# A router with stationary weights, a gather from the norm's weighted rows, and low parts made by GpSimd

## What is computed

```python
x = layer_norm(ALPHA * x + h, ln_g[i, 0], ln_b[i, 0])     # h: output of the windowed attention
logits = (xf @ w_router).astype(jnp.float32)              # 256 x 8
top_val, top_idx = lax.top_k(logits, TOP_K)               # 2 of 8 experts
top_w = jax.nn.softmax(top_val, axis=-1)
for e in range(N_EXPERTS):
    h = jax.nn.silu(xf @ w_gate[e]) * (xf @ w_up[e])      # 1024 x 3584
    out = out + gates[:, e:e + 1] * (h @ w_down[e])
```

## Time and profile before

| | us |
|---|---|
| median of 3 runs | 2149.47 |
| lowest and highest | 2147.61, 2150.2 |
| the profiled execution, its own time | 2145.25 |
| span of its profile | 2143.4 |
| granted TensorE clock, mean | 0.995 |
| TensorE busy | 2104.2 |
| VectorE busy | 1755.8 |
| ScalarE busy | 1508.5 |
| GpSimd busy | 397.3 |

### The profile page before, as it was taken

One profiled execution on the slowest core, in us unless ns is written; L12 is line 12 of the kernel. 1 busy time (PEld: TensorE's weight loads), 2 busy tenths in 40 slices (PEclk: granted clock), 3 DMA queues, 4 the chain that ended last, 5 costly groups with the idle time before them and its releaser, 6 DMA issues.

```text
span 2143.4 us, 32785 instructions
## 1 busy us (share of the span) xinstructions
PE 2104.2 (98%) x12715; PEld 1820.4 (85%) x12715; DVE 1755.8 (82%) x2194; ACT 1508.5 (70%) x2018; POOL 397.3 (19%) x354
## 2 busy tenths in 40 slices
PE   9999999989999999999999999999999999999998
PEld 8888888878888888888888888888899888999887
DVE  6756766879999999999999999986699676689775
ACT  5644444666887888888888888876578955668964
POOL 1511000001002000000000000000558700277820
PEclk9999999999999999999999999999999999999999
DMA  8225956439999999999999999994656465655561
GB/s 286 100 66 130 278 183 181 162 100 353 361 361 387 394 387 394 380 391 365 395 360 395 378 382 375 382 361 134 203 164 205 153 233 164 190 179 176 179 211 60
DMA packets 297418, 564.58 MB, mean 263 GB/s; under 512 B 19600, under 2 KB 113576, under 8 KB 297256
## 3 DMA queue, kind: packets, MB, share of 16 engines
q1 hardware_dynamic: 285328, 527.60, 69.7%
q0 software_dynamic: 11824, 34.77, 5.9%
q10 hardware_dynamic: 104, 0.04, 0.0%
HBM read 548.32 MB, written 14.02 MB: 262 GB/s over the span
## 4 chain that ended last, share of the span: by engine, by line
PE 92%; DVE 4%; ACT 2%; issue 1%; SPq 1%; DMA 0%; DVEq 0%; ACTq 0%
PE bank L953 26%; PE bank L955 26%; PE bank L954 25%; PE bank L1549 4%; PE bank L959 2%; PE bank L1550 2%; PE bank L1953 1%; PE bank L1130 1%; DVE parts L2857 1%; PE bank L1913 1%; PE bank L1934 0%; PE bank L1926 0%; DMA raw<-in_a_w_in_dram 0%; DVE work L2996 0%; PE bank L1876 0%
## 5 line engine op out<-in xcount | busy, mean ns | idle before, releaser
L2857 DVE TENSOR_TENSOR parts<-raw,parts 128x1024 fp32r<-128x1024 f32 x701 | 849.8, 1228 | 274.6 <-ACT parts L2086 249.5
L2086 ACT CAST parts<-raw 128x1024 fp32r<-128x1024 f32 x701 | 730.8, 1048 | 395.3 <-PE bank L955 313.9
L2857 DVE TENSOR_TENSOR fast<-raw,fast 128x1024 fp32r<-128x1024 f32 x302 | 361.9, 1218 | 24.2 <-ACT fast L2086 7.4
L2086 ACT CAST fast<-raw 128x1024 fp32r<-128x1024 f32 x302 | 316.4, 1052 | 84.6 <-PE bank L955 78.1
L953 PE MATMUL bank<-parts,cols 128*128 128x512 f32 x868 | 344.2, 397 | 3.2 <-DVE cols L2911 1.9
L955 PE MATMUL bank<-parts,cols 128*128 128x512 f32 x868 | 338.5, 390 | 0.0
L954 PE MATMUL bank<-parts,cols 128*128 128x512 f32 x868 | 338.2, 390 | 0.0
L953 PE MATMUL bank<-cols,parts 128*128 128x256 f32 x1040 | 300.4, 289 | 0.0
L954 PE MATMUL bank<-cols,parts 128*128 128x256 f32 x1040 | 294.8, 283 | 0.0
L955 PE MATMUL bank<-cols,parts 128*128 128x256 f32 x1040 | 294.8, 283 | 0.0
L953 PEld LDWEIGHTS bank<-cols,parts 128*128 128x128 f32 x1040 | 199.3, 192 | 4.0 <-issue 2.0
(11 more groups left out here) (457 smaller groups left out, 3454.1 us busy)
## 6 DMA issues: line engine op xcount, KB each, us to landing
raw<-in_moe_w_gate_dram SPq DMA_DIRECT2D x112, 1024.0 KB, 9.4
raw<-in_moe_w_up_dram SPq DMA_DIRECT2D x112, 1024.0 KB, 8.9
raw<-in_moe_w_down_dram SPq DMA_DIRECT2D x112, 1024.0 KB, 9.2
raw<-in_w_in_dram SPq DMA_DIRECT2D x76, 1024.0 KB, 5.4
raw<-in_a_w_in_dram SPq DMA_DIRECT2D x11, 1024.0 KB, 11.7
raw<-in_ffn_w_gate_dram SPq DMA_DIRECT2D x11, 1024.0 KB, 5.5
raw<-in_ffn_w_up_dram SPq DMA_DIRECT2D x11, 1024.0 KB, 5.5
raw<-in_ffn_w_down_dram SPq DMA_DIRECT2D x11, 1024.0 KB, 5.0
```

The lines of the kernel that those rows point to most:

```text
L2086: a.copy(dst[0], src).then_inc(*up(o + "hi", x))
L2857: v.tensor_tensor(dst[1], src, dst[0].bitcast(F32), ALU.subtract).then_inc(*up(o + "lo", x))
```

## The change

1. The router's weights become the stationary operand: high and low parts lie side by side in one slot (16 columns for each of the 8 blocks of the width), and the tokens move, high and low parts in one matmul of 256 columns. That is 8 matmuls for each tile, into banks 5 and 0. The result has the experts on the partitions. VectorE copies it to SBUF, and TensorE turns it with two small float32 products for each tile, with a 16 x 8 matrix `fold` that also adds the high and low rows; VectorE copies that to the logits.
2. The gather of expert 0 reads P, not X. The selection matrix for it holds 1/deviation in place of 1 (`sel_sd`, `spots`), so it waits for the counts and for nothing of the norm's rows; the norm's offset is transposed into the gather's two banks ahead of time (8 transposes). Banks 4 and 6 are taken.
3. The counts are three products in place of five, and three float32 products of the identity, written to bank 1 and read by nobody, stand before `sel` and behind the counts (`keep_busy`).
4. The norm's rows are written by VectorE within the norm: tile 1's right behind its diagonal, tile 0's behind tile 1's low parts.
5. The low parts of eight weight pieces (the five late ones, `GATE_LO`, and the three behind the router's, `ROUTE_LO`) are GpSimd's. GpSimd takes the three after its four DMAs of X, and loads the next norm's constants only when the gather is done, since their buffer now lies where P does.
6. On VectorE the two low parts of the gather come before `route_ends`; `picked(0)` and `ids(0)` move from expert step 0 to step 1.

```diff
+    GATE_LO = LATE_LO[2]
+    ROUTE_LO = list(W.after.get(T_rt, ()))
...
+        for y in GATE_LO:
+            piece_lo(y)
         gp.wait_ge(*at("rows", 2, 0))
         gp.wait_ge(*at("lo_x", 2, 0, 1))
         for d in (x_d, f_d):
             gp.dma_start(d[0:T, :].rearrange("(a p) d -> p a d", p=128), X).then_inc(*up("x_away", 0, by=16))
             gp.dma_start(d[T:, :], X[:, 0, :]).then_inc(*up("x_away", 0, by=16))
+        for y in ROUTE_LO:
+            piece_lo(y)
+        gp.wait_ge(*at("gathered", 0, 1))
         ln_rows(N4.gb, 1, 1, 3)
...
-        narrow(bank[5], T_rt, 8, 5, TILES[2], 2)
-        busy[5] = ("logits",)
+        def logits():
+            pe.wait_ge(*at(lo_name(T_rt), T_rt))
+            both = v3(router_slot(), 8)
+            for t, b in zip(TILES[2], (5, 0)):
+                claim(b)
+                pe.wait_ge(*at("lo_x", 2, t, 1))
+                o = bank[b][0:16, 0:T].rearrange("p (q c) -> p q c", q=2)
+                for k in range(8):
+                    k_ = pe.matmul(o, both[:, k, :], v3(XT_both[:, k, :], 2)[:, :, t * 128:(t + 1) * 128], start=k == 0, stop=k == 7, skip_group_check=True)
...
+            for t in TILES[2]:
+                pe.wait_ge(*at("logit_rows", t))
+                for q in range(2):
+                    k_ = pe.matmul(bank[7][:, 32 + 8 * t:40 + 8 * t], N4.lT[:, t * T + q * 128:t * T + q * 128 + 128], N4.fold, start=q == 0, stop=q == 1)
+            k_.then_inc(*up("logits_turned"))
+        logits()
+
+        for hf in range(2):
+            b = gather_bank(MAIN, 0, hf)
+            claim(b)
+            for j in range(4):
+                cs = slice((4 * hf + j) * 128, (4 * hf + j + 1) * 128)
+                pe.matmul(bank[b][:, j * 128:(j + 1) * 128], N3.gb[:, 1, cs], ident, start=j == 0, stop=False, is_transpose=True, skip_group_check=True)
+        claim(1)
+        keep_busy(3, 1, ident)
         pe.wait_ge(*at("sel"))
...
+                if e == 0 and o == MAIN:
+                    pe.wait_ge(*at("spots"))
+                    for j in range(4):
+                        kk = 4 * hf + j
+                        for t in range(2):
+                            k = pe.matmul(bank[b][:, j * 128:(j + 1) * 128], N3.P[:, t, kk * 128:(kk + 1) * 128], N4.P_[:, 1, t, :], start=False, stop=(j, t) == (3, 1), skip_group_check=True)
...
-                if i == 0:
-                    for y in rest[:between]:
-                        lo(W, MAIN, y)
-            del rest[:between]
+                if n == 2 and i == 0:
+                    norm_rows(n, gb, P, (t,))
             for i, t in enumerate(TILES[n]):
                 for g in range(2):
                     cols_lo(n, XT, t, g, 6 + g - 2 * t)
                 for y in (rest[:1], rest[1:])[i]:
                     lo(W, MAIN, y)
+                if n == 2 and i == 0:
+                    norm_rows(n, gb, P, TILES[n][1:])
...
-        norm_rows(2, N3.gb, N3.P)
+        v.tensor_tensor(N4.sel_sd, sel[:, :, 0:1], v3(LT[:, 0:16], 2)[:, :, 5:6], ALU.mult).then_inc(*up("dve"))
+        v.wait_ge(*at("dve"))
         v.wait_ge(*at("counts"))
+        for t in range(2):
+            k = v.tensor_scalar(N4.P_[:, 1, t, :], C(C_IOTA), bank[7][:, 8 * t:8 * t + 1], N4.sel_sd[:, t, :], ALU.is_equal, ALU.mult)
+        k.then_inc(*up("spots"))
...
             picks(0)
+            gather(0, 0)
+            gather(0, 1)
             if side:
                 route_ends()
-                for y in rt_next[:3]:
-                    lo(W_, o, y)
-            gather(0, 0)
-            if side:
-                for y in rt_next[3:]:
-                    lo(W_, o, y)
-            gather(0, 1)
```

More of the change, by code:

```diff
@@ L84 @@
     "dve_merge": ("yb", "merged"),
-    "dve_expert": ("picks", "lo_g", "hh", "lo_h", "y", "sum", "ids"),
+    "dve_expert": ("spots", "picks", "lo_g", "hh", "lo_h", "y", "sum", "ids"),
     "dve_o_expert": ("o_picks", "o_lo_g", "o_hh", "o_lo_h", "o_y", "o_sum"),
@@ L431, in _program @@
         pass
-    N4.gb = v3(take(2 * D), 2)
-    N4.fa = v3(take(2 * D), 2)
-    N4.xg = [tuple(v3(cols_[:, q, 1024 * a:1024 * a + 1024], 8) for q in range(2)) for a in range(2)]
-    sg_hh = take(4 * 512)
-    N4.sg, N4.hh = v3(sg_hh[:, 0:1024], 2), v3(sg_hh[:, 1024:2048], 2)
     N4.P_ = v4(take(2 * 256), 2, 2)
@@ L442, in _program @@
     N4.ids = take(2).bitcast(U32)
+    N4.gb = v3(take(2 * D), 2)
+    N4.fa = v3(take(2 * D), 2)
+    N4.xg = [tuple(v3(cols_[:, q, 1024 * a:1024 * a + 1024], 8) for q in range(2)) for a in range(2)]
+    sg_hh = take(4 * 512)
+    N4.sg, N4.hh = v3(sg_hh[:, 0:1024], 2), v3(sg_hh[:, 1024:2048], 2)
+    N4.lT = sg_hh[0:16, 0:512]
     N4.rows, N4.ys = N4.fa[:, 0, :], N4.fa[:, 1, :]
@@ L452, in _program @@
     N4.left = v4(rt[:, 192:224], 2, 2)
+    N4.fold, N4.sel_sd = rt[0:16, 32:40], v3(rt[:, 40:42], 2)
     N4.g01 = v3(rt[:, 128:132], 2)
@@ L683, in raw_view, with router_slot @@
         return raw[:, c % RAW, 0:a * b].rearrange("p (a b) -> p a b", a=a)
+    def router_slot():
+        i = W.pieces[T_rt]["slot"]
+        return (parts_[:, i, 0, :] if i < PIECES else more[i - PIECES])[:, 0:128]
     def piece_view(W_, x):
@@ L688, in piece_view @@
         i = W_.pieces[x]["slot"]
+        if W_ is W and x == T_rt:
+            return src, tuple(v3(router_slot(), 8)[:, :, 8 * q:8 * q + 8] for q in range(2))
         if i >= PIECES:
@@ L694, in _program, with gather_bank @@
     MAIN, MORE = "", "o_"
+    def gather_bank(o, e, hf):
+        if o == MAIN and e == 0:
+            return (4, 6)[hf]
+        return 6 if (e, hf) == (0, 1) else 7
     def sync_program(sp):
@@ L1706, in tensor_program @@
-        pe.matmul(bank[7][:, 16:24], ones, sel[:, 1, :], start=False, stop=True).then_inc(*up("counts"))
+        def logits():
[7 more added lines that the diff above has]
+                    k_ = pe.matmul(o, both[:, k, :], v3(XT_both[:, k, :], 2)[:, :, t * 128:(t + 1) * 128], start=k == 0, stop=k == 7, skip_group_check=True)
+                k_.then_inc(*(up("logit_cols", t) if t == TILES[2][0] else up("used", T_rt)))
+                busy[b] = ("logit_rows", t)
+            claim(7)
+            for t in TILES[2]:
[3 more added lines that the diff above has]
+            k_.then_inc(*up("logits_turned"))
@@ L1707, in tensor_program @@
+        pe.matmul(bank[7][:, 8:24], ones, sel[:, 0, :].unsqueeze(1).broadcast_to([128, 2, 8]), start=False, stop=False, skip_group_check=True)
+        pe.matmul(bank[7][:, 16:24], ones, sel[:, 1, :], start=False, stop=True, skip_group_check=True).then_inc(*up("counts"))
+        keep_busy(3, 1, ident)
         busy[7] = ("ranked",)
@@ L2860, in after @@
             for y in W_.after.get(x, ()):
-                if W_ is W2 or y not in late and y not in POOL_LO:
+                if W_ is W2 or y not in late and lo_name(y) == "lo":
                     lo(W_, o, y)
@@ L2919, in norm_rows, with residual_norm @@
                 k.then_inc(*up("rows", n, t))
-        def residual_norm(n, gb, P, ends, x_in=None, between=0):
-            rest = list(LATE_LO[n])
+        def residual_norm(n, gb, P, ends, x_in=None):
+            rest = list(LATE_LO[n]) if n < 2 else []
             if n == 0:
@@ L3500, in experts @@
                     gather(e + 1, g - 4)
-                if side and n == 0:
+                if side and n == 1:
                     ids(0)
```

63 lines of the change are left out of this document (34 added, 29 removed).

## The result

The changed kernel takes 2160.21 us (median of 7 runs, 2155.88 to 2162.58) against 2147.61 us of the kernel before (7 runs beside it). By the medians it is 12.6 us slower; the ratio is 1.0053 [1.0041, 1.0064], which is 11.4 us. Forecast were 0.9 us faster, and 2152.5 was the upper end of the range. The profiled execution took 2160.21, span 2158.3.

A forecast was written before the change was run, and what follows sets the result against it. TensorE, busy 98%, bounds the kernel, so only the 19.57 us ahead of the experts can shrink: 7.2 us gained less 6.3 lost to GpSimd overlap is 0.9, from 2149.47 to 2148.6 us; range 2142.0 to 2152.5.

The forecast's parts named there:

- Norm held by GpSimd: Third norm: VectorE's ln_p and diagonal wait for GpSimd's pieces, so TensorE's tile 0 starts 5.4 us later.
- half clock on tile 0's 16 instructions: Norm on TensorE: half clock behind the idle gap, on about half of the 16 instructions, loses 0.9 us.
- Router: Router up to the logits: 16 matmuls of 256 columns in place of 32 narrow ones, gain 1.3 us.
- Norm rows off the selection: Selection to gather: without the norm rows on VectorE the counts come last, gain 2.6 us.
- Gather at full clock and nothing late behind it: Expert 0's gather: 3.6 us against 6.25, gain 2.65; low part of its first half no longer late, gain 0.6.
- Sum of the gains: Router, selection, gather and what follows it: 7.2 us together, first gate product at 486.3 before losses.
- Small instructions of the selection beside GpSimd: Selection's 8 to 16 column VectorE instructions: taken as 0, though up to 2.3 us for each one caught.
- margin of 0.4 us: Selection: spots due at 488.6, GpSimd's ROUTE_LO at about 489; 0.4 us later and spots is held.
- rivals, 2: Selection: ROUTE_LO holds spots and picks, 2 or 3 times 2.3 us on top; 2153.2 to 2155.5 us, chance 0.12.
- sign against the clock step: Gather: if it takes over 5 us, the claim of 3.6 us at clock 1.00 is wrong.
- The prediction's own rule: VectorE beside GpSimd: two SBUF operands, or a wide SBUF-to-SBUF instruction, wait until GpSimd's running instruction ends.
- GpSimd's pieces were never late: Weights: GpSimd's pieces slow but not late; a TensorE wait for a weight piece after 493 us would refute it.

The follow-up runs named there:

- e8_gaps: Changed kernel with three norm low parts on GpSimd behind tile 0's diagonal, two on VectorE, norm rows later, ROUTE_LO on VectorE: 2147.22 us, ratio 0.9986.
- e6_route_late: Changed kernel plus one wait: GpSimd starts ROUTE_LO only when expert 0's selection (picks) is written; 2148.27 us, ratio 0.9999.
- e11_early_picks: e8_gaps with picks(1), expert 1's selection, moved right behind route_ends on VectorE; 2146.56 us, ratio 0.9985.
- e1_vector_lows: Changed kernel with all eight low parts given back to VectorE, the rest of the change kept; 2150.21 us, ratio 1.0001.
- e3_route_vector: Changed kernel with ROUTE_LO given back to VectorE and GATE_LO kept on GpSimd; 2148.56 us, ratio 1.0001.
- e10_no_filler: e3_route_vector without the two groups of three idle identity products (keep_busy) around the counts; 2150.58 us, ratio 1.0011.
- e5_before_gpsimd: Kernel before with only the eight low parts moved to GpSimd, router, gather and norm rows as before; 2160.67 us, ratio 1.0054.
- base_again: Meant as a second profile of the kernel before; by mistake the changed kernel ran unaltered; 2155.98 us (one run).

## Why the prediction was wrong

Step by step, with the measured value behind the predicted one:

- Norm held by GpSimd: 5.4 predicted, 8.51 - 3.63 = 4.9 measured; half clock on tile 0's 16 instructions 0.9 predicted, measured about 1.6 (483.22 to 486.62, against 1.78). The mechanism and the instructions (second half of `ln_p`, diagonal) are those named.
- Router: gain 1.3 predicted. In `e8_gaps`, where hardly anything is held, B is 6.22 against 6.87; with the step that the kernel before still needs behind its copy, some 0.9. In `e6_route_late` B is 7.18; without the 1.6 of half clock this is 5.6, a gain of 1.3.
- Norm rows off the selection: 2.6 predicted, 4.07 - 1.62 = 2.45 measured in `e6_route_late`.
- Gather at full clock and nothing late behind it: 2.65 + 0.6 = 3.25 predicted, 6.90 - 3.59 = 3.31 measured in the same kernel. There the clock did stay up. In the changed kernel it fell to 0.50 at 494.3, in the wait for held instructions, and E is 5.12.
- Sum of the gains: 7.2 predicted, 5.4 in the stretch of `e8_gaps`, where the clock stays up. The prediction also let every microsecond at the first gate product arrive at the end; in `e8_gaps` and `e11_early_picks` 1.9 and 1.7 of it were given back by 660 us. This term was mis-sized, but it isn't what put the time outside the range.
- Small instructions of the selection beside GpSimd: taken as 0. **This is the step that failed.** C and D are 5.33 + 5.34 in the changed kernel and 1.78 + 1.62 in `e6_route_late`, which differs by one wait: 7.3 us. E adds 1.5 through the clock, B 0.3. That is 9.1 of the 9.5 us between the two profiles' spans (2158.3 and 2148.8). The medians of the two lie 11.9 us apart; the rest isn't traced to anything.
- Behind the first gate product the changed kernel falls back by another 1.95 us against the kernel before, up to 1879 us. Up to 1440 us it is 0.9, without any wait, and the same 0.9 to 1.0 is in `e1_vector_lows`, `e3_route_vector`, `e6_route_late` and `e10_no_filler`, whatever their start; `e5_before_gpsimd`, with the old router and gather, has none. So it comes with the rest of the change and not with GpSimd. No run tells from which part; the prediction had no term for it.

The prediction's reason for the 0 was that piece 5 and the DMAs lie beside most of the selection. This place was right: logits to `ROUTE_LO` were 2.8 us in the forecast and are 493.49 - 490.68 = 2.81. But it took DMA issues as harmless and left `spots` a margin of 0.4 us ahead of `ROUTE_LO`. The copy held beside the issues cost 2.2 us, more than that margin, and then the small instructions ahead of `spots` were caught in turn: 1.73, 2.01 and 2.31 us. Even in `e6_route_late`, where the copies lose only 0.3 each, `spots` starts (493.67) just ahead of the end of the last DMA issue (493.71), so the margin was in truth next to nothing.

Of the rivals, 2 comes nearest, but it isn't what happened. Its heading (`ROUTE_LO` catches the selection) is right, and its condition (`spots` comes 0.4 us later) was met. The instructions that it names are not: neither `spots` nor `picks` was held (0.61 and 0.60 us for two each), and the sign that the prediction set for it, selection matrices of over 1 us, didn't show. The four that were held are smaller ones ahead of them, which no sum of the prediction has. Its time, 2153.2 to 2155.5, was too low as well. The sign against the clock step (a gather of over 5 us) did show, 5.37; the cause was the wait for held instructions, since with that wait gone the gather ran at 1.00.

The prediction's own rule spoke of two operands in SBUF, "or a wide one from SBUF to SBUF". The word "wide" was tested by no row: the 16-column TENSOR_SCALARs are the same operation, SBUF to SBUF, as the diagonal, which it did walk. And a margin of 0.4 us, on a sum with terms of 5 us, shouldn't have been priced at a chance of 0.12.

That `e3_route_vector` and `e6_route_late` come so near the forecast (0.5 us in the stretch for 0.9) owes something to luck: in the norm the hold was 0.5 us shorter and the half clock 0.7 us longer than predicted.

Held up too: GpSimd's pieces were never late (no wait for a weight piece behind the first gate product in the changed kernel). And a single profile says little of where a stretch lies: 470.30 for the norm's start is the earliest of all profiles here.

## What to carry to other kernels

An instruction of another engine costs what it makes wait, not what it takes: put GpSimd's SBUF work in a stretch in which VectorE reads PSUM or idles, by a wait if need be, and walk every VectorE instruction of a latency chain against it, however small. Don't count on a narrow margin between two queues; price the chain of what follows if it is lost, since one held instruction can push the next into the same trap. And when a start is moved forward, ask whether the stream behind it can follow; here about two of five microseconds were given back.

## What the hardware did that was not expected

- VectorE instructions of 2 to 16 columns took up to 4.91 us beside GpSimd's subtractions, against 0.15 to 0.18 alone, and one of 16 x 8 elements 1.37 against 0.13; size gives no protection. What one loses is the rest of GpSimd's running instruction, and in one case the next two as well.
- Beside fills of GpSimd (0.95 each) a TENSOR_SCALAR of 16 columns took 2.11 us, a two-operand instruction of 512 columns its usual 0.7.
- Beside GpSimd's DMA issues copies of 2 to 4 columns took 0.4 to 0.5 us with nothing queued behind the issues (`e3_route_vector`, `e6_route_late`), and 2.40 and 2.01 us with a subtraction queued behind (the changed kernel, `base_again`). Others beside them were free (0.17).
- The clock fell to 0.50 behind gaps of 2.12 and 1.60 us in the router (`e1_vector_lows`) and stayed at 1.00 with gaps of 0.57, 0.57 and 1.13 us (`e8_gaps`). Ahead of the third norm it was 0.50 for 17.1 us in one execution of the changed kernel and for 6.8 in another.
